# Scores and masked products of a gated linear attention as two 64-column blocks in two column groups

## The reference

```python
def gla_chunked(q, k, v, glog, s0):
    C = GLA_CHUNK                                  # 64
    ...
    att = jnp.einsum('bnihk,bnjhk->bnhij', qc * jnp.exp(g - g_mid), kc * jnp.exp(g_mid - g))
    att = jnp.where(jnp.tril(jnp.ones((C, C), dtype=bool)), att, 0.0)
    o_intra = jnp.einsum('bnhij,bnjhv->bnihv', att, vc)
    ...
    o_inter = jnp.einsum('bnihk,bnhkv->bnihv', qc * jnp.exp(g), s_prev)
    o = (o_intra + o_inter).reshape(b, s, h, dv).astype(v.dtype)
```

## Time and profile before

| what | value |
|---|---|
| median of 3 runs | 2058.43 us (2058.36 to 2059.71) |
| the profiled execution, its own time | 2058.17 us |
| span of that execution | 2056.0 us |
| PE busy | 1911.4 us, 93% |
| DVE busy | 1243.5 us, 60% |
| ACT busy | 1069.3 us, 52% |
| mean granted TensorE clock | 0.941 |

### The profile page before, as it was taken

How to read it: one execution, slowest core, us unless ns; L and a number is a source line. 1 busy time by engine, 2 the same in 40 slices (tenths; PEclk the granted TensorE clock), 3 DMA queues, 4 the chain that set the end, 5 groups by cost and what they waited for, 6 DMA issues and landing times.

```text
span 2056.0 us, 25790 instructions
## 1 busy us (share of the span) xinstructions
PE 1911.4 (93%) x10392; PEld 1579.1 (77%) x10392; DVE 1243.5 (60%) x1379; ACT 1069.3 (52%) x1368; POOL 43.6 (2%) x38
## 2 busy tenths in 40 slices
PE   6999889979999998898887999999999999999995
PEld 4889456868888786788567788888888888888784
DVE  3241751452222334442654889898989898888886
ACT  4232642352222224433534677677777777676764
POOL 0000000000000000000000020000000000000000
PEclk9999885889999999899967899999999999999997
DMA  8211633212222222212802899998989998989894
GB/s 336 103 62 63 226 145 121 73 49 105 83 103 102 82 103 82 89 62 103 307 22 82 319 350 368 338 368 343 366 342 364 344 362 346 360 343 343 336 339 163
DMA packets 61530, 441.87 MB, mean 215 GB/s; under 512 B 6836, under 2 KB 6964, under 8 KB 8288
## 3 DMA queue, kind: packets, MB, share of 16 engines
q1 hardware_dynamic: 60032, 436.23, 56.3%
q10 hardware_dynamic: 1120, 3.28, 0.4%
q0 software_dynamic: 256, 0.66, 0.1%
HBM read 439.10 MB, written 1.05 MB: 214 GB/s over the span
## 4 chain that ended last, share of the span: by engine, by line
PE 84%; DVE 10%; ACT 3%; DMA 2%; issue 1%; SPq 0%; DVEq 0%; ACTq 0%
PE psum L1446 72%; DMA raw<-units 2%; PE psum L1782 2%; PE psum L1658 1%; PE psum L1664 1%; DVE act_lo L1088 1%; PE psum L1641 1%; PE psum L1825 1%; DVE row_max L1168 1%; PE psum L1463 1%; PE psum L1798 1%; ACT probs L773 1%; DVE states L1199 1%; PE psum L1469 1%; DVE y_mix L1237 1%
## 5 line engine op out<-in xcount | busy, mean ns | idle before, releaser
L1331 DVE TENSOR_TENSOR w_lo<-raw,w_hi 128x2048 fp32r<-128x2048 f32 x136 | 311.0, 2289 | 52.3 <-ACT w_hi L922 51.6
L922 ACT ACTIVATE w_hi<-raw 128x2048 fp32r<-128x2048 f32 x136 | 260.8, 1919 | 109.0 <-PE psum L1446 106.4
L1024 DVE TENSOR_TENSOR w_lo<-raw,w_hi 128x1024 fp32r<-128x1024 f32 x130 | 153.3, 1221 | 197.9 <-ACT w_hi L628 197.9
L1446 PE MATMUL psum<-w_hi,xt_hi 128*128 128x512 f32 x596 | 234.2, 393 | 2.7 <-DVE xt_lo L1336 2.7
L1446 PE MATMUL psum<-w_hi,xt_lo 128*128 128x512 f32 x596 | 233.4, 392 | 0.0
L1446 PE MATMUL psum<-w_lo,xt_hi 128*128 128x512 f32 x596 | 233.2, 391 | 0.0
L1331 DVE TENSOR_TENSOR w_lo<-raw_more,w_hi 128x2048 fp32r<-128x2048 f32 x90 | 206.0, 2290 | 35.7 <-ACT w_hi L922 35.3
L628 ACT ACTIVATE w_hi<-raw 128x1024 fp32r<-128x1024 f32 x130 | 130.2, 1051 | 157.2 <-PE psum L1446 151.6
L922 ACT ACTIVATE w_hi<-raw_more 128x2048 fp32r<-128x2048 f32 x90 | 172.8, 1920 | 75.4 <-PE psum L1446 75.4
L1446 PE MATMUL psum<-act_hi,w_hi 128*128 128x512 f32 (+1 forms) x544 | 208.8, 384 | 2.1 <-DVE act_lo L1088 1.9
L1446 PE MATMUL psum<-act_lo,w_hi 128*128 128x512 f32 (+1 forms) x544 | 207.6, 382 | 0.0
(11 more groups left out here) (260 smaller groups left out, 3636.1 us busy)
## 6 DMA issues: line engine op xcount, KB each, us to landing
raw<-units SPq DMA_DIRECT2D x295, 1024.0 KB, 4.9
raw_more<-units SPq DMA_DIRECT2D x120, 1024.0 KB, 4.9
X<-ctx_in ACTq DMA_DIRECT2D x1, 1024.0 KB, 16.6
X<-x_in ACTq DMA_DIRECT2D x1, 1024.0 KB, 23.3
out<-X SPq DMA_DIRECT2D x1, 1024.0 KB, 4.1
const<-const_in ACTq DMA_DIRECT2D x1, 520.0 KB, 9.6
rope<-rope_in POOLq DMA_DIRECT2D x2, 256.0 KB, 5.6
wsm<-wsm_in ACTq DMA_DIRECT2D x1, 288.0 KB, 26.9
```

What stands on the lines that cost most here:

```text
L922: act.activation(w_place(m)[0], raw_place(m), ACT.Copy).then_inc(esem("w_high"), 1)
L1024: ins = dve.tensor_tensor(w_lo[:, i % RING, part], raw[:, i % RING, part], w_hi[:, i % RING, part].bitcast(F32), ALU.subtract)
L1331: dve.tensor_tensor(lo, raw_place(m), hi.bitcast(F32), ALU.subtract).then_inc(esem("w_ready"), 1)
L1446: ins = pe.matmul(dst, lhs(a), rhs(b), start=first and n == 0, stop=last and n == 2)
```

## The change

Both products are cut at the chunk border. The score job makes, for each direction, two 64x64 blocks on the diagonal where it made one 128x128 block; the blocks off the diagonal are no longer computed (the masked copy never took them). The first block writes PSUM partitions 0 to 63, the second 64 to 127. The masked product uses 64 of the 128 columns of `Am` at a time, with all 128 rows, and writes half of the partitions with each. What is stored in `Am` and all other instructions stay.

```diff
                     for d in range(2):
                         dp = 2 * d + pair
-                        ins = pe.matmul(bank(key)[:, d * P:(d + 1) * P], gexp[r, 1, dp, t * P:(t + 1) * P],
-                                        gexp[r, 0, dp, t * P:(t + 1) * P], start=True, stop=True)
+                        for half in range(2):
+                            a = half * CHUNK
+                            c = slice(t * P + a, t * P + a + CHUNK)
+                            ins = pe.matmul(bank(key)[a:a + CHUNK, d * P + a:d * P + a + CHUNK], gexp[r, 1, dp, c],
+                                            gexp[r, 0, dp, c], start=True, stop=True)
                     ins.then_inc(filled, 1)
...
                     for d in range(2):
-                        pe.matmul(bank(key)[:, 0:P], Am[:, (i - 1) % 2, d, :], gv[:, t, h * P:(h + 1) * P],
-                                  start=d == 0, stop=False, skip_group_check=True)
+                        for half in range(2):
+                            rows = slice(half * CHUNK, (half + 1) * CHUNK)
+                            pe.matmul(bank(key)[rows, 0:P], Am[:, (i - 1) % 2, d, rows], gv[:, t, h * P:(h + 1) * P],
+                                      start=d == 0, stop=False, skip_group_check=True)
```

## The result

The changed kernel takes 2040.94 us (median of 4 runs, 2040.22 to 2042.73) where the kernel before takes 2059.07 us beside it: ratio 0.991, 95% interval 0.9893 to 0.9927. That is 18.1 us. The prediction was 15.0 us less, 2043.4 us.

What follows compares the result with a forecast made beforehand. PE at clock 0.50 was taken to bound the items; 13.3 us from scores plus 1.7 from masked products made 15.0 less, 2043.4 us, with 2038.5 to 2051.5 for 8 in 10.

Steps and rivals of the forecast that it cites:

- PE is the bound and the clock is 0.50: GLA items of both layers: PE runs almost without idle time at 1.2 GHz, so records cost twice their full-clock time.
- A record costs by its moving columns, two column groups run side by side: Score and masked products: score records 0.107 us each, four deep per group, so 0.43 us where 0.85 stood.
- Rival (A): Score products: both column groups share one weight path, scores stay 0.85 us, total 2051.3; chance 0.16 including partly unhidden loads.
- Rival (B): Masked products: halves run one after another, 20.4 us more, 5.4 slower in sum, 2063.8 us; chance 0.06.
- Equal shape: Between state products and scores: the shape change (0.13 us) and unhidden first weight load (0.16) fall away.
- Weight loads and order: Score records: loads hidden on the same rows, groups not in strict program order; otherwise 3.8 us lost, 2047.2 us.
- Which runs count: Score runs before PE waits gain nothing: 12 in layer 0 and 6 in layer 1 gain 0.73 us each, 13.3 in all.
- The masked product's share: Masked products in both layers: a shorter first weight load saves 0.10 us in each of 17 runs, 1.7 us.
- the clock behind the items: After the items: moved work can meet a clock rise or fall differently; 2 us allowed either way.
- Rival (C): Within the items: with fewer gaps the clock may rise from 0.50 to 1.00, 16 us more, 2027 us; chance 0.07.

## Why the prediction was right, step by step

**PE is the bound and the clock is 0.50.** Right. Both layers' items gave 14.9 us, and the stretches after still have 0.50.

**A record costs by its moving columns, two column groups run side by side.** Right, and shown from both sides: eight records of 64 columns in one group are 0.107 each, in two groups they take half; the same with 128 rows in the masked product (1.89 against 1.05 us). Rival (A) had 0.22 us for each pair of score records in the changed kernel; they take 0.11. It is refuted also by the run with all 128 moving columns, which is 0.44 us a turn longer with the same weights. The run with one group doesn't speak to (A), which has 0.11 for a load by itself; it shows that the groups do run side by side. Rival (B) is refuted by the masked product's 1.05 us, and its price over the changed kernel was 19.6 us where 20.4 was named; against the kernel before that made 3.3 us slower, not 5.4.

**Equal shape.** Right: 0.30 of the 0.73 us of a score run remains when the halved columns are taken back. One of the prediction's reasons for it was misread, though. It took the first two score jobs, 8 records in 0.72 us at full clock, for two jobs one behind the other without a gap. At the step of 0.11 us that each job has there, eight in a row would need 0.88. In the trace they start in pairs (1034.74 and 1034.75, then 1034.92 and 1034.97, and so on): items 0 and 1 are heads 0 and 1, on different rows, and ran side by side. The conclusion held, but that row didn't support it.

**Weight loads and order.** The Trainium skill, "TensorE: Matmul & The Clock Gate", Part 3, "The mechanism", lists loads as hidden only across different rows, and matmuls as started in program order; the text ahead of that list also lets a load into a background weight buffer run ahead. This case's trace disagrees with both points of the list, and agrees with what the text says of a background buffer as far as hidden loads go: score records at steps of 0.107 us on the rows of the state products leave no room for bare loads. And score records start at 297.80, before a state record at 298.02 that precedes them.

**Which runs count.** Right: the waits for `mod_row` are 0.51 and 2.38 us (about 0.6 and 2.4 forecast), and taking them away brought 2.47 us within the items. The masked product's share, 1.7 us, was 1.8 alone.

**What came beside.** The measured 18.1 and 16.2 us exceed the 14.9 of the items. The prediction allowed 2 us either way for the clock behind the items; the two profiles of the changed kernel differ by 4.6 us in span at equal items, so this allowance was too small. The surplus is therefore no part of the mechanism that was shown, and that the second median, 2043.10, lies so near the forecast 2043.4 is in part luck: its 16.2 us hold 1.3 that the items don't. Whether the shorter items make one course of the clock behind them more likely wasn't settled: the time after layer 1's items is 984.0 to 985.5 us in six of the seven profiles with changed scores and the old order of heads, and 988 in the three with the old scores.

**Rival (C)**, a clock that rises within the items, did not happen with this change. It happened with the heads reordered, and brought more than the records themselves: of the 24.7 us by which the items got shorter in the second profile of that order, the records are at most 18 x 0.42 = 7.6.

## What to carry to other kernels

When a product is block-diagonal, cut it so that its pieces fall in different column groups, and give it the row and column shape of its neighbours in PE's order: here 0.43 us of each 0.73 came from the cut and 0.30 from the shape. Price the cut by moving columns per group, and look next for a neighbour with the same shape on the other rows, because that hides a whole run (with another shape it hid nothing). Count only runs that aren't followed by a wait that starts before them. A masked product of 64 rows and 64 columns, which would give all of a turn one shape, was not tried: jobs of one shape on different rows ran interleaved here, so a state product on the other rows could then write the partitions of the masked product it adds to with nothing that orders the two. What would come of that isn't shown.

## What the hardware showed that wasn't expected

Four blocks of 64x64 (two column groups, two row groups) run at once without cost to each other: a 0.43 us or even a 0.85 us run of scores hides beside 0.85 us of state products. The trace of the kernel before shows it already, unnoticed: the 128 records of line 1627 (128 moving columns, 0.11 us each at full clock, both halves of the rows in turn) took 4.59 us, three at a time, where two column groups allow two. The share of time in which PE counts as busy doesn't tell the granted clock: at 95% busy it stayed at 0.50 for the 60 us of layer 0's items in the changed kernel, and at 100% for the 19 us of layer 1's. In all four profiles in which both row groups had work it rose within the items, about 5 us or more before their end; in one of the others, the run with both masked halves in one group, it rose 0.8 us before their end, in the rest not at all. Why it rises where it does isn't shown: in the two profiles of the order alone it first rises 18.1 and 8.7 us after layer 0's items begin. In this kernel products that nobody uses, in an idle part of the array, made the program no slower; its times lay within 3.1 us (4 runs) instead of 21.6 (6 runs), which so few runs leave open to chance.
